# Gate projections of two branch stages: seven products of quarter blocks for eight, with sums of token quarters made during the second silu pass

## The chip, the cores and the metric

One core of a Trainium2 chip runs the whole program. The metric is the device time of one execution in microseconds. Five engines work side by side, each with its own instruction stream, ordered by semaphores only: TensorE (PE, matmuls from SBUF into PSUM), VectorE (DVE), ScalarE (ACT), GpSimd (POOL) and SyncE (SP, which here issues nearly all DMAs, in order). PSUM has eight banks of 128 x 512 floats.

## The reference, cut to what matters

The program is a two-layer hybrid block followed by a second block, on 1024 tokens of width 1024, all in float32. The change touches one part of the second block: in each of its two branches an output `o` is multiplied by a silu, projected, and gated by a sigmoid. All four factors but `o` are columns of one projection `h @ w_in`.

```python
h = rms_norm(x, norm_pre[i])
(aq, ak, av, az, dq, dk, dv, db, da, dz, gate_att, gate_dn) = split_cols(h @ w_in[i])
...
y_att = (o_att * jax.nn.silu(az)) @ w_br_att[i]
...
y_dn = (o_dn * jax.nn.silu(dz)) @ w_br_dn[i]
mix = (jax.nn.sigmoid(gate_att) * y_att + jax.nn.sigmoid(gate_dn) * y_dn) @ w_out[i]
```

`h` is 1024 x 1024; `az`, `dz`, `gate_att` and `gate_dn` are 1024 columns each; the branch weights and `w_out` are 1024 x 1024.

## The kernel before, in words

`stage_branch` (line 2653) computes one branch and is called twice: stage a for attention (tiles named `bhsa`, `bringa`, ...) and stage n for the delta branch (`bhsn`, ...). Everything is held transposed, features on the 128 partitions: `hT` as eight chunks of 128 features x 1024 tokens, in DRAM as `hTd`.

Float32 accuracy comes from splitting. Each operand is rounded to the PE's fast format (the high part, by ACT for weights and by DVE for `h`), the remainder is formed by POOL or DVE (the low part), and a product takes three matmuls: high x high, high x low, low x high. A 128x512 weight slice is one piece of work: it is loaded by SP into a staging tile (line 2726), rounded by ACT into a ring of four (line 2811), its low part is made by POOL (line 2840), and PE (line 2779) multiplies its four blocks of 128 columns with both halves of the tokens: eight units, one for each PSUM bank, three matmuls each.

The stage is six passes of eight pieces: two silu passes (four blocks of 128 output features each), two gate passes, two branch passes. In a pass every piece adds one chunk of 128 input features to all eight banks. In the first silu pass the chunks of `hT` are loaded into two buffers, rounded by DVE (line 2858) and completed by POOL (line 2833) into `hs`, where all of `h` stays for four passes. After a silu pass ACT takes the silu of each bank (line 2799) and DVE multiplies it into `yT` (line 2869). After a gate pass ACT writes the sigmoids straight from PSUM into `mixT` (line 2801). Before the branch passes `yT` is rounded into `hs` (DVE line 2873, POOL line 2837). After a branch pass DVE multiplies each bank with its gates (line 2897 in stage a, 2901 in stage n) and in stage n adds the other branch's result (line 2904), which SP has read into `yT` in one 4 MB DMA (line 2740). The result is stored (line 2750).

The order is written out by hand. SP loads a slice once POOL has used the staging tile three slices back; ACT rounds a slice once PE has used the ring entry four back:

```python
for n in range(DONE, SLICES):
    ...
    if n >= RING:
        wait_slice(act, n - RING)
    act.activation(ring[:, n % RING, 0, :], slice_in(n)[:, :], ACT.Copy).then_inc(s_hi, 1)
    c, kc = divmod(n - LEAD, KC)
    if 0 <= c < GATED and kc == KC - 1:
        activate(c)
```

The functions of a pass follow two pieces behind the rounding (`LEAD`). The first piece of each stage (and in stage n the raw inputs of the second) is prepared by the stage before. During the last branch pass stage a prepares inputs of the conv stage (`conv`), and stage n those of the last projection (`ahead`).

## Time and profile before

| | |
|---|---|
| median of 3 runs | 3266.35 us (3263.31 to 3268.9) |
| profiled execution | 3268.52 us |
| its span, first to last instruction | 3266.7 us |
| mean granted clock of TensorE | 0.971 |
| stage a | about 1746 to 2010 us of the span |
| stage n | about 2806 to 3068 us of the span |

The span is what the engines' records cover; the execution is 1.8 us longer. Busy times overlap between engines and matmuls overlap among themselves, so a matmul's mean duration is longer than the distance between two starts. The granted clock is the share of 2.4 GHz that TensorE ran at.

### The profile page before, as it was taken

How to read it: one execution, taken by the hardware profiler on the slowest of the kernel's cores; microseconds unless marked ns; L12 is line 12 of the kernel's file. 1: busy time of each engine (PE TensorE's matmuls, PEld its weight loads, DVE VectorE, ACT ScalarE, POOL GpSimd, SP SyncE). 2: the span in 40 equal slices, each digit the busy share in tenths (PEclk: the TensorE clock that was granted, in tenths of full speed). 3: DMA queues.
4: the chain of work that ended last, by engine and by line, in shares of the span. 5: the costliest groups of instructions: out<-in, count | busy, mean ns of one | idle time of the engine just before them, and what ended most of it. 6: DMA issues, size and time to landing. Idle time of an engine off the chain costs nothing. (4 is left out here: it accounts for less than half of the span.)

```text
span 3266.7 us, 43916 instructions
## 1 busy us (share of the span) xinstructions
PE 3016.7 (92%) x16017; PEld 2466.8 (76%) x16017; DVE 2044.6 (63%) x3738; ACT 1408.0 (43%) x2790; POOL 1175.9 (36%) x1306
## 2 busy tenths in 40 slices
PE   7999989989999899798999999997989888999998
PEld 5678867756887667587887887787877788788787
DVE  6889976576998756676773004677857788301244
ACT  3356557224664661335663211455434553321232
POOL 5226532232363223522004242235443445524331
PEclk8999999989999999899999999999999999999999
DMA  8422333541233245410002124124241232412342
GB/s 294 136 55 84 116 107 103 166 162 51 69 97 108 93 137 168 133 52 1 1 6 90 51 62 144 29 53 99 71 123 39 65 94 76 163 47 102 116 155 71
DMA packets 229609, 309.41 MB, mean 95 GB/s; under 512 B 41199, under 2 KB 142447, under 8 KB 227217
## 3 DMA queue, kind: packets, MB, share of 16 engines
q1 hardware_dynamic: 217874, 285.62, 28.7%
q10 hardware_dynamic: 11520, 20.98, 1.8%
q8 instruction: 128, 2.10, 0.3%
q14 instruction: 87, 0.71, 0.1%
HBM read 244.01 MB, written 62.52 MB: 94 GB/s over the span
## 5 line engine op out<-in xcount | busy, mean ns | idle before, releaser
L1027 PE MATMUL psum<-qs,hT 128*128 128x512 f32 x1248 | 284.5, 389 | 1.4 <-POOL qs L1112 1.4
L1027 PEld LDWEIGHTS psum<-qs,hT 128*128 128x128 f32 x1248 | 233.8, 188 | 51.8 <-POOL qs L1112 3.5
L2779 PE MATMUL psum<-bhsn,bringn 128*128 128x512 f32 x1056 | 241.1, 390 | 2.4 <-DVE bhsn L2861 1.5
L2779 PE MATMUL psum<-bhsa,bringa 128*128 128x512 f32 x1056 | 240.1, 389 | 2.9 <-POOL bringa L2840 2.9
L2779 PEld LDWEIGHTS psum<-bhsn,bringn 128*128 128x128 f32 x1056 | 197.9, 188 | 45.2 <-DVE bmixn L2901 2.2
L2779 PEld LDWEIGHTS psum<-bhsa,bringa 128*128 128x128 f32 x1056 | 198.1, 188 | 44.4 <-issue 3.3
L3158 PE MATMUL psum<-hTs,cws 128*128 128x512 f32 x960 | 230.2, 396 | 0.0
L3158 PEld LDWEIGHTS psum<-hTs,cws 128*128 128x128 f32 x960 | 179.3, 190 | 36.3
L1192 DVE TENSOR_SCALAR_CACHE_REDUCE junk<-score,cand 128x384 uint8<-128x384 f32 x248 | 186.8, 810 | 2.2
L1907 PE MATMUL psum<-w_out,oys 128*128 128x512 f32 x768 | 181.1, 398 | 6.9 <-POOL oys L1974 4.7
L1907 PEld LDWEIGHTS psum<-w_out,oys 128*128 128x128 f32 x768 | 147.1, 192 | 41.1 <-POOL oys L1974 5.9
L3521 DVE SCALAR_TENSOR_TENSOR cacc<-craw,taps,cacc 128x1024 f32<-128x1024 f32 x96 | 159.0, 1657 | 3.4
L1074 ACT ACTIVATE sign<-key,wbias 128x896 bf16<-128x896 f32 x124 | 134.4, 1085 | 54.8 <-POOL wbias L1118 45.2
L2202 PE MATMUL psum<-fw,fhs 128*128 128x512 f32 x552 | 135.3, 405 | 17.5 <-DVE fhs L2301 10.5
L2202 PEld LDWEIGHTS psum<-fw,fhs 128*128 128x128 f32 x552 | 106.3, 195 | 43.4 <-DVE fhs L2301 10.7
L1654 DVE CUSTOM_DVE_ANT_0 pm<-psum,score 128x384 f32<-128x384 f32 (+5 forms) x96 | 85.0, 887 | 60.1 <-PE psum L1438 45.3
L2840 POOL TENSOR_TENSOR bringa<-bstga,bringa 128x512 fp32r<-128x512 f32 x47 | 63.6, 1357 | 141.9 <-ACT bringa L2811 141.9
L2533 DVE TENSOR_REDUCE amx<-psum 128x1 f32<-128x1024 f32 x64 | 78.3, 1224 | 57.2 <-PE psum L2404 57.2
L1527 ACT ACTIVATE pm<-pm,mn 128x384 f32<-128x384 f32 (+7 forms) x128 | 99.1, 774 | 29.9 <-DVE mn L1654 29.5
L1112 POOL TENSOR_TENSOR qs<-stg,qs 128x512 fp32r<-128x512 f32 x72 | 98.8, 1385 | 34.2 <-ACT qs L1048 30.9
L2840 POOL TENSOR_TENSOR bringn<-bstgn,bringn 128x512 fp32r<-128x512 f32 x46 | 60.3, 1315 | 140.8 <-ACT bringn L2811 140.8
L1438 PE MATMUL psum<-ks,qs 128*128 128x512 f32 (+3 forms) x384 | 104.6, 384 | 4.6 <-DVE mn L1654 4.3
(564 smaller groups left out, 7134.0 us busy)
## 6 DMA issues: line engine op xcount, KB each, us to landing
stg<-in_w_in SPq DMA_DIRECT2D x88, 256.0 KB, 2.7
score<-in_w_ada SPq DMA_DIRECT2D x32, 512.0 KB, 4.3
pj<-ptmp ACTq DMA_DIRECT2D x64, 256.0 KB, 2.1
dlb<-blocks SPq DMA_DIRECT2D x32, 512.0 KB
dlb<-in_w_in SPq DMA_DIRECT2D x20, 512.0 KB, 3.9
wa<-in_w_ada SPq DMA_DIRECT2D x8, 1024.0 KB, 12.7
ostg<-in_w_out SPq DMA_DIRECT2D x16, 512.0 KB, 6.0
x<-ozb SPq DMA_DIRECT2D x16, 512.0 KB, 3.0
```

Of the source, the lines that this page charges most:

```text
L1027: mm = pe.matmul(bank(m), lhs, rhs, start=(first and x == 0), stop=(last and x == 2))
L1074: act.activation(sign[:, wide[b]], key[:, wide[b]], ACT.Sign, bias=wbias[:, b:b + 1], accum_out=wcnt[:, b:b + 1]).then_inc(s_cnt[b], 1)
L1112: pool.tensor_tensor(dst[:, 1, :], stg[n % STAGING][:, :], dst[:, 0, :].bitcast(F32), ALU.subtract).then_inc(s_lo, 1)
L1192: ins = dve.tensor_scalar(junk[:, SC_OFF[b]:SC_OFF[b + 1]], spans[b], s1, 0.0, op, ALU.add, accum_out=cnt[:, b:b + 1])
L1438: mm = pe.matmul(ps[:, 2 * (n % 2) + c // HALF, 0:m], h.qs[:, hd, i * P:(i + 1) * P], h.ks[:, x, c:c + m], start=(x == 0), stop=(x == 1))
L1527: act.activation(pm[n % PM][:, 0:keys], pm[n % PM][:, 0:keys], ACT.Exp, bias=mn[:, n:n + 1], scale=-1.0, accum_out=rs[:, n:n + 1]).then_in ...
L1907: mm = pe.matmul(ps[:, 2 * (n % SLOTS) + half, :], ys[n % YS][:, a, kc, :], w[:, b, kc, half * HALF:(half + 1) * HALF], start=(kc == 0 and ...
L2202: mm = pe.matmul(ps[:, 2 + u % 3, :], hs[n % 2][:, i, kc, :], w[c][:, j, kc, :], start=(kc == 0 and x == 0), stop=(kc == KC - 1 and x == 2))
L2779: mm = pe.matmul(ps[:, m, :], w[:, a, fs], h, start=(j == 0 and x == 0), stop=(j == KC - 1 and x == 2))
L2840: pool.tensor_tensor(ring[:, n % RING, 1, :], slice_in(n)[:, :], ring[:, n % RING, 0, :].bitcast(F32), ALU.subtract).then_inc(s_lo, 1)
L3158: mm = pe.matmul(ps[:, u % 4, :], w, h, start=(kc == 0 and x == 0), stop=(kc == KC - 1 and x == 2))
L3521: link(dve.scalar_tensor_tensor(acc[:, :], r[:, s:s + SEQ], taps[:, c, s:s + 1], acc[:, :], ALU.mult, ALU.add))
```

## The change

In the four passes that project gate columns (two in each stage), the work is cut into four pairs of 128-column blocks. For one pair, the weights form a 2 x 2 arrangement: feature half (chunks 0 to 3, chunks 4 to 7) by block; `a11` and `a21` are the first half's two blocks, `a12` and `a22` the second half's. `h` forms another: feature half by token half, `b11`, `b12` (first feature half, early and late tokens), `b21`, `b22`. Instead of eight products of quarters, seven are made:

| product | weights | tokens | bank |
|---|---|---|---|
| A11 | a11 | b11 | x |
| S2 | a21 + a22 - a11 | T2 = b22 - T1 | y |
| S1 | a21 + a22 | T1 = b12 - b11 | z |
| A12 | a12 | b21 | x, added |
| S3 | a11 - a21 | T3 = b22 - b12 | y, added |
| S4 | a12 - (a21 + a22 - a11) | b22 | z, added |
| A22 | a22 | T4 = b21 - T2 | w |

Each product is four chunks x three matmuls of 128x128 weights with 512 tokens, all into one bank. The results of a pair are A11 + A12; A11 + S2 + S1 + S4; A11 + S2 + S3 + S1; and A11 + S2 + S3 + A22. ACT copies A11 and S1 out of PSUM while they are still to be added to (`keep`), DVE makes the sums, ACT takes the sigmoids.

What goes with it:
- DVE forms the weight sums of a pair from raw weights (three after the third product's sums of the pair before, one after S2). SP loads a pair as two DMAs of 512 KB; ACT and POOL split each of the seven 128x512 weights as before, in the same ring of four.
- The token sums T1 to T4 are made in the second silu pass, for chunks i and i + 4 together, in four rounds. `hTd` is read again (eight chunks, 512 KB each). DVE makes four differences, ACT rounds three parts, DVE makes the low parts. T2 is written over the late half of chunk i in `hs`. The first pair waits for the fourth round (`s_T`).
- The gates no longer go to `mixT`, whose place T1 and T3 take: each pair's four tiles are stored to a DRAM tensor `gated` (256 KB each), and the whole is read back into `mixT` as one 4 MB DMA at the start of the branch passes, issued behind the fifth branch slice. The first multiplication waits for it (`s_gl`).
- Four `hT` buffers for two, two silu tiles for three. Chunk 0 is now loaded and split into `hs` too. Slice staging shares memory with the raw pairs.
- In stage a the three loads for `conv` get buffers of their own, without the wait between the second and the third.

The diff, cut to its core:

```diff
+    HK, PROD, PAIRS = KC // 2, 7, 4
+    RING, STAGING, LEAD, TMP, U, HST = 4, 3, 2, 2, 8, 4
+    PAIR0, BR0 = 2 * KC, 2 * KC + PROD * PAIRS
...
+    F_A11, F_S2, F_S1, F_A12, F_S3, F_S4, F_A22 = range(PROD)
...
+            def load_pair(j):
...
+                if j == 1:
+                    sp.wait_ge(s_lo, PAIR0 - DONE)
+                if j >= 2:
+                    sp.wait_ge(s_lo, item(j - 2, PROD - 1) + 1 - DONE)
+                for half in range(2):
+                    sp.dma_start(pair_raw(j)[:, half].rearrange("p k f q -> p k (f q)"),
+                                 win[:, HK * half:HK * (half + 1), columns_of(j):columns_of(j) + 2 * P]
+                                 ).then_inc(s_k[(j + 1) % 2], 16)
+            def store_gates(j):
+                for i, tl in enumerate((0, 1, 2, 3)):
+                    f, half = home(j, i)
+                    sp.wait_ge(s_out, 4 * j + i + 1)
+                    sp.dma_start(t["gated"][:, f, half * HALF:(half + 1) * HALF], tile[j % 2][tl][:, :]
+                                 ).then_inc(s_gst[j % 2], 16)
...
+            for n, i in ((KC + 1, 0), (KC + 3, 1), (KC + 4, 2), (KC + 5, 3)):
+                for v in range(KC + 2 if i == 1 else n, n + 1):
+                    load_silu(v)
+                if i == 2:
+                    load_pair(0)
+                for kc in (i, i + HK):
+                    load_chunk(chunk(kc, True))
+            for n in range(KC + 6, PAIR0):
+                load_silu(n)
+            load_pair(1)
+            load_pair(2)
+            store_gates(0)
+            load_pair(3)
+            store_gates(1)
+            for n in range(BR0, ITEMS):
+                c, kc = pass_of(n)
+                if n == BR0:
+                    sp.wait_ge(s_lo, item(PAIRS - 2, PROD - 1) + 1 - DONE)
+                if n >= BR0 + STAGING:
+                    sp.wait_ge(s_lo, n - STAGING + 1 - DONE)
+                load_slice(n, wbr[:, kc, (c - 2) * HALF:(c - 1) * HALF])
+                if n == BR0 + STAGING - 1:
+                    store_gates(PAIRS - 2)
+                if n == BR0 + STAGING + 1:
+                    store_gates(PAIRS - 1)
+                    sp.wait_ge(s_prod, PROD * PAIRS)
+                    for q in range(2):
+                        sp.wait_ge(s_gst[q], 128)
+                    sp.dma_start(mixT[:, :, :], t["gated"]).then_inc(s_gl, 16)
...
+            def product(n):
+                j, p = pair_of(n)
+                x, y, z, w = (4 * (j % 2) + i for i in range(4))
+                bank = {F_A11: x, F_S2: y, F_S1: z, F_A12: x, F_S3: y, F_S4: z, F_A22: w}[p]
+                opens = p in (F_A11, F_S2, F_S1, F_A22)
+                pe.wait_ge(s_lo, n + 1 - DONE)
+                if j == 0 and p == F_A11:
+                    pe.wait_ge(s_T, HK)
...
+                if p == F_A12:
+                    pe.wait_ge(s_kept, 2 * j + 1)
+                if p == F_S3:
+                    pe.wait_ge(s_u, 5 * j + 1)
+                if p == F_S4:
+                    pe.wait_ge(s_kept, 2 * j + 2)
+                for kc in range(HK):
+                    for i, (a, b) in enumerate(((0, 0), (0, 1), (1, 0))):
+                        mm = pe.matmul(ps[:, bank, :], ring[:, n % RING, a, kc * P:(kc + 1) * P], moving(p, b, kc),
+                                       start=(opens and kc == 0 and i == 0), stop=(kc == HK - 1 and i == 2),
+                                       skip_group_check=True)
+                mm.then_inc(s_prod, 1)
...
+            def t_hi(i):
+                a, b = hst[chunk(i, True) % HST], hst[chunk(i + HK, True) % HST]
+                act.wait_ge(s_traw, i + 1)
+                wait_item(act, KC + i)
+                act.activation(T13[:, 0, i, :], a[:, :], ACT.Copy)
+                act.activation(T4[:, 0, i, :], b[:, 0:HALF], ACT.Copy)
+                act.activation(hs[:, 0, i, HALF:SEQ], b[:, HALF:SEQ], ACT.Copy).then_inc(s_thi, 1)
...
+            def keep(j, p):
+                act.wait_ge(s_prod, PROD * j + p + 1)
+                if p == F_A11:
+                    if j == 0:
+                        act.wait_ge(s_T, HK)
+                    wait_tiles(act, j)
...
+            def activate(j, i):
+                act.wait_ge(s_u, 5 * j + 2 + i)
+                if i == 0:
+                    act.wait_ge(s_prod, PROD * j + F_A12 + 1)
+                src = ps[:, 4 * (j % 2), :] if i == 0 else tile[j % 2][i][:, :]
+                act.activation(tile[j % 2][i][:, :], src, ACT.Sigmoid).then_inc(s_out, 1)
+            def after(n):
+                j, p = pair_of(n)
+                if p in (F_A11, F_S1):
+                    keep(j, p)
+                if p == F_S3:
+                    activate(j, 0)
+                    activate(j, 1)
+                if p == F_S4:
+                    activate(j, 2)
+                if p == F_A22:
+                    activate(j, 3)
...
+            for n in range(DONE, ITEMS):
+                hi(n)
+                if KC + RING <= n < PAIR0:
+                    t_hi(n - KC - RING)
+                if n in (KC - 1 + LEAD, PAIR0 - 1 + LEAD):
+                    for m in range(U):
+                        silu(U * (n // KC - 1) + m)
+                if PAIR0 <= n - LEAD < BR0:
+                    after(n - LEAD)
...
+            def make_t(i):
+                a, b = wait_chunk(dve, i, True), wait_chunk(dve, i + HK, True)
+                early, late = slice(0, HALF), slice(HALF, SEQ)
+                link(dve.tensor_tensor(a[:, early], a[:, late], a[:, early], ALU.subtract))
+                link(dve.tensor_tensor(a[:, late], b[:, late], a[:, late], ALU.subtract))
+                link(dve.tensor_tensor(b[:, late], b[:, late], a[:, early], ALU.subtract))
+                dve.tensor_tensor(b[:, early], b[:, early], b[:, late], ALU.subtract).then_inc(s_traw, 1)
+                dve.wait_ge(s_thi, i + 1)
+                dve.tensor_tensor(T13[:, 1, i, :], a[:, :], T13[:, 0, i, :].bitcast(F32), ALU.subtract)
+                dve.tensor_tensor(T4[:, 1, i, :], b[:, early], T4[:, 0, i, :].bitcast(F32), ALU.subtract)
+                dve.tensor_tensor(hs[:, 1, i, late], b[:, late], hs[:, 0, i, late].bitcast(F32),
+                                  ALU.subtract).then_inc(s_T, 1)
+            def weight_sums(j):
+                r = pair_raw(j)
+                a11, a21, a22 = r[:, 0, :, 0, :], r[:, 0, :, 1, :], r[:, 1, :, 1, :]
+                dve.wait_ge(s_k[(j + 1) % 2], 32 * (j // 2 + 1))
+                if j:
+                    dve.wait_ge(s_lo, item(j - 1, F_S4) + 1 - DONE)
+                dve.tensor_tensor(S[0][:, :, :], a21, a22, ALU.add).then_inc(s_S, 1)
+                dve.wait_ge(s_S, 4 * j + 1)
+                dve.tensor_tensor(S[1][:, :, :], S[0][:, :, :], a11, ALU.subtract).then_inc(s_S, 1)
+                dve.tensor_tensor(a21, a11, a21, ALU.subtract).then_inc(s_S, 1)
+            def last_weight_sum(j):
+                dve.wait_ge(s_lo, item(j, F_S2) + 1 - DONE)
+                dve.tensor_tensor(S[1][:, :, :], pair_raw(j)[:, 1, :, 0, :], S[1][:, :, :], ALU.subtract).then_inc(s_S, 1)
...
+            def after_second(j):
+                tl, y = tile[j % 2], ps[:, 4 * (j % 2) + 1, :]
+                dve.wait_ge(s_prod, PROD * j + F_S2 + 1)
+                dve.wait_ge(s_kept, 2 * j + 1)
+                wait_tiles(dve, j)
+                dve.tensor_tensor(tl[2][:, :], y, tl[0][:, :], ALU.add).then_inc(s_u, 1)
+            def after_third(j):
+                tl, y = tile[j % 2], ps[:, 4 * (j % 2) + 1, :]
+                dve.wait_ge(s_prod, PROD * j + F_S3 + 1)
+                dve.tensor_tensor(tl[3][:, :], y, tl[0][:, :], ALU.add).then_inc(s_u, 1)
+                dve.wait_ge(s_kept, 2 * j + 2)
+                dve.wait_ge(s_u, 5 * j + 2)
+                dve.tensor_tensor(tl[1][:, :], tl[3][:, :], tl[1][:, :], ALU.add).then_inc(s_u, 1)
+            def after_last(j):
+                tl, z, w = tile[j % 2], ps[:, 4 * (j % 2) + 2, :], ps[:, 4 * (j % 2) + 3, :]
+                dve.wait_ge(s_prod, PROD * j + F_S4 + 1)
+                dve.tensor_tensor(tl[2][:, :], z, tl[2][:, :], ALU.add).then_inc(s_u, 1)
+                dve.wait_ge(s_prod, PROD * j + F_A22 + 1)
+                dve.tensor_tensor(tl[3][:, :], w, tl[3][:, :], ALU.add).then_inc(s_u, 1)
...
+            for kc in range(DONE, KC):
+                h_hi(kc)
+            a = wait_chunk(dve, 0)
+            dve.wait_ge(s_used, DONE)
+            link(dve.tensor_copy(hs[:, 0, 0, :], a[:, :]))
+            dve.tensor_tensor(hs[:, 1, 0, :], a[:, :], hs[:, 0, 0, :].bitcast(F32), ALU.subtract).then_inc(s_h0, 1)
+            silus(range(U))
+            for i in range(HK):
+                make_t(i)
+                if i == 1:
+                    weight_sums(0)
+            silus(range(U, 2 * U))
+            for j in range(PAIRS):
+                after_second(j)
+                last_weight_sum(j)
+                if j == PAIRS - 1:
+                    dve.wait_ge(s_sm, 2 * U)
+                    dve.wait_ge(s_prod, PROD * j + F_S2 + 1)
+                    for kc in range(HK):
+                        y_hi(kc)
+                after_third(j)
+                if j + 1 < PAIRS:
+                    weight_sums(j + 1)
+                after_last(j)
+            for kc in range(HK, KC):
+                y_hi(kc)
```

## Rows read from the trace of the kernel before

**Rows 1.** page, busy time of the engines over the whole span.

```profile
PE 3016.7 (92%) x16017; PEld 2466.8 (76%) x16017; DVE 2044.6 (63%) x3738; ACT 1408.0 (43%) x2790; POOL 1175.9 (36%) x1306
```

**Rows 2.** windows: us; PE, PEld, DVE, ACT, POOL busy; clock; DMA; GB/s.

```profile
1792.30:1835.80 43.50, 43.50 (x193) 36.02 (x193) 5.43 (x9) 9.62 (x17) 10.28 (x8) 1.00 0.19 49
1835.80:1879.30 43.50, 43.50 (x193) 36.02 (x193) 1.81 (x3) 10.88 (x18) 10.29 (x8) 1.00 0.19 49
...
2933.90:2977.40 43.50, 43.50 (x194) 36.03 (x193) 4.86 (x7) 9.60 (x17) 17.39 (x11) 1.00 0.18 49
```

**Rows 3.** timeline, first gate pass of stage a: start us, us, engine, line.

```profile
1841.53 38.24 PE L2779 MATMUL psum<-bhsa,bringa 128*128 128x512 f32 x168
...
1847.22 0.63 ACT L2811 ACTIVATE bringa<-bstga 128x512 fp32r<-128x512 f32 x1 [4.81 <-PE psum L2779]
1847.93 1.29 POOL L2840 TENSOR_TENSOR bringa<-bstga,bringa 128x512 fp32r<-128x512 f32 x1 [4.14 <-ACT bringa L2811]
```

**Rows 4.** timeline, PE in the conv stage, 24 matmuls to a bank.

```profile
2054.19 11.05 PE L3158 MATMUL psum<-hTs,cws 128*128 128x512 f32 x48
```

**Rows 5.** groups, stage a: count | busy us, mean ns | idle before it.

```profile
L2869 DVE TENSOR_TENSOR attT<-attT,btmpa 128x512 f32<-128x512 f32 x16 | 10.9, 693 | 53.4 <-ACT btmpa L2799 53.4
...
L2892 DVE TENSOR_TENSOR ahead_w<-bhsta,ahead_w 128x1024 fp32r<-128x1024 f32 x2 | 2.5, 1226 | 0.1
...
L2811 ACT ACTIVATE bringa<-bstga 128x512 fp32r<-128x512 f32 x47 | 29.2, 631 | 177.5 <-PE psum L2779 140.4 <-DMA bstga<-in_w_in 29.3 <-DMA bstga<-in_w_br_att 7.8
...
L3311 ACT ACTIVATE hTs<-ahead_h 128x2048 fp32r<-128x2048 f32 x1 | 1.9, 1917 | 23.8 <-PEq L124 23.8
...
L2799 ACT ACT_TABLE_LOAD x1 | 1.3, 1283 | 0.0
...
L2840 POOL TENSOR_TENSOR bringa<-bstga,bringa 128x512 fp32r<-128x512 f32 x16 | 20.6, 1292 | 61.7 <-ACT bringa L2811 61.7
...
L2837 POOL TENSOR_TENSOR bhsa<-attT,bhsa 128x1024 fp32r<-128x1024 f32 x3 | 7.2, 2406 | 0.0
```

**Rows 6.** timeline, end of stage n's first branch pass.

```profile
3016.71 0.69 DVE L2901 TENSOR_TENSOR bmixn<-psum,bmixn 128x512 f32<-128x512 f32 x1 [38.07 <-PE psum L2779]
3016.80 1.29 POOL L2840 TENSOR_TENSOR bringn<-bstgn,bringn 128x512 fp32r<-128x512 f32 x1 [1.97 <-ACT bringn L2811]
3017.43 1.20 DVE L2904 TENSOR_TENSOR bmixn<-bmixn,odT 128x512 f32<-128x512 f32 x1
```

**Rows 7.** page, DMA issues: count, KB each, median us to landing.

```profile
dlb<-in_w_in SPq DMA_DIRECT2D x20, 512.0 KB, 3.9
...
bstga<-in_w_in SPq DMA_DIRECT2D x31, 256.0 KB, 2.7
...
bhsta<-hTd SPq DMA_DIRECT2D x8, 512.0 KB, 3.6
...
od<-dodT SPq DMA_DIRECT2D x16, 256.0 KB, 2.5
...
odT<-mixd SPq DMA_DIRECT2D x1, 4096.0 KB, 12.2
```

**Rows 8.** timeline, stage n: the 4 MB read, the slice behind it rounded.

```profile
2998.71 0.33 SPq L2740 DMA_DIRECT2D odT<-mixd  x1
...
3011.58 1.31 ACT L2811 ACTIVATE bringn<-bstgn 128x512 fp32r<-128x512 f32 x2 [11.18 <-DMA bstgn<-in_w_br_dn]
```

**Rows 9.** timeline, PE in stage n: a pass starts; after waiting for DVE.

```profile
2934.23 0.39 PE L2779 MATMUL psum<-next_bh_hi,bringn 128*128 128x512 f32 x1
...
3027.63 39.06 PE L2779 MATMUL psum<-bhsn,bringn 128*128 128x512 f32 x171 [0.37 <-DVE bmixn L2901]
```

**Rows 10.** timeline, PE after a gap: stage a; the stage behind n.

```profile
1754.37 38.36 PE L2779 MATMUL psum<-bhsa,bringa 128*128 128x512 f32 x168 [2.91 <-POOL bringa L2840]
...
3070.27 11.94 PE L4456 MATMUL psum<-mw,mms 128*128 128x512 f32 x44 [3.58 <-PEq L2666]
```

**Rows 11.** windows, the 4 us behind that gap.

```profile
3070.00:3074.00 4.00, 3.73 (x10) 3.01 (x11) 0.00 (x0) 0.97 (x2) 0.50 (x2) 0.57 0.60 196
```

More of the change, by code:

```diff
@@ L2723, in _ @@
-                off = {"silu": silu_off, "gate": gate_off, "branch": 0}[what]
-                off += part * HALF
-                src = (wbr if what == "branch" else win)[:, kc, off:off + HALF]
-                sp.dma_start(stg[n % STAGING][:, :], src).then_inc(s_w[n % STAGING], 16)
-                if c == 0 and y_in is not None and kc >= HG:
-                    for f in range(2 * (kc - HG), 2 * (kc - HG) + 2):
-                        sp.dma_start(yT[:, f, :], y_in[:, f, :]).then_inc(s_y[f // 4], 16)
@@ new lines, in _ @@
+            for n in range(LOADED, KC):
+                if y_in is not None and n == HG:
+                    sp.wait_ge(k.od_last[0], 32)
+                    sp.wait_ge(k.od_last[1], 32)
+                load_chunk(chunk(n, False))
+                load_silu(n)
+                if y_in is not None and n >= HG:
+                    for f in range(2 * (n - HG), 2 * (n - HG) + 2):
+                        sp.dma_start(yT[:, f, :], y_in[:, f, :]).then_inc(s_y[f // 4], 16)
+            load_chunk(chunk(0, False))
@@ L2738, in _ @@
+                if conv and c == 3 and kc == 3:
+                    sp.dma_start(hst[2][:, :], t["hTd"][:, 0, :]).then_inc(s_chi, 16)
+                if mix_in is not None and c == 2 and kc == KC - 1:
                     sp.wait_ge(s_ylo, KC)
```

323 lines of the change are left out of this document (207 added, 116 removed).

## The prediction

> **What bounds the kernel now.** I read the page's busy line first: TensorE (PE) is busy for 92% of the span, no other engine over 63% [rows 1]. That is an average, so I went to the windows, one for each pass of the two branch stages (called a and n here, after the tag in their tile names). In each of the four gate passes and in stage a's second silu pass PE is busy for the whole 43.50 us, at a granted clock of 1.00, while VectorE (DVE), ScalarE (ACT) and GpSimd (POOL) are busy for 2 to 17 us and the DMA share is 0.17 to 0.19 (the silu pass, the first and the last gate pass are shown) [rows 2]. Then the timeline of one gate pass: ACT's roundings come 5.44 us apart (4.81 of waiting for PE and 0.63), and POOL's low part follows at once; the two feeders wait for PE, never PE for them [rows 3]. So here a matmul saved is time saved, as long as the feeders keep their lead. The price of a matmul is the spacing of starts and not the mean of 389 ns, which overlaps: 43.50 us / 192 = 0.2266 us.
>
> **The matmuls.** A gate pass is 8 pieces x 8 units x 3 = 192 matmuls; two stages with two passes each make 768. After: 2 stages x 4 pairs x 7 products x 12 = 672, all with the same 128x128 weights and 512 moving columns. Removed: 96 x 0.2266 = 21.75 us, on the path. What is new is that twelve follow each other in one PSUM bank, where before three did. The conv stage does just that (24 in a row): 48 in 11.05 us, less the 0.39 of the last, over 47 gaps: 0.227 us [rows 4]. Cost nothing; bounds 0 and, if each of the 56 products paid the 0.16 us between 0.39 and 0.227 once for a drain, 9 us. I take 0: pieces follow each other today with a wait between them and no gap: 168 in 38.24 us [rows 3].
>
> **Feeding the pairs.** A product lasts 12 x 0.2266 = 2.72 us, a pair 19.03. Per pair POOL has 7 x 1.29 = 9.0 us, ACT 7 roundings, two copies and four sigmoids at 0.63, 8.2 us, DVE nine operations at 0.69, 6.2 us [rows 3, 5]. All are below 19, so only the order can hurt. Counted from the pair's start, the products end at 2.7, 5.4, 8.2, 10.9, 13.6, 16.3, 19.0. The tight place is the next pair's first two weights. DVE ends its two sums after the third sum's product (S3) at 15.1; ACT, whose two sigmoids wait for them, ends those at 15.8 and rounds the next A11 by 16.4; POOL has the low part at 17.8, needed at 19.0. For the next product DVE must first pass three weight sums (to 17.3) and the sum of S4 (18.0), then ACT a sigmoid and a rounding (19.35), POOL a low part (20.7), needed at 21.8: 1.1 us in hand. The third product's weight comes at 22.5, needed at 24.5. In a two-input DVE operation on SBUF that meets a POOL one the row is 1.20 us for 0.69 [rows 6], and one such meeting falls into the three sums: 0.6 left. Stall 0; bounds 0 and, with all five DVE operations at 1.20, 2.55 - 1.1 = 1.5 us at each of the six inner boundaries, 9 us. I take 0.
>
> In those same rows DVE starts at 3017.43 inside POOL's 3016.80 to 3018.09 and ends 0.54 us after it, so here the later one seems to wait until the other is through. The Trainium skill (SBUF — State Buffer, Who interferes with whom) says so as a rule: such an operation and a GpSimd read take one shared port in turn and the second "fully blocks". By it the third weight sum would wait for the whole of POOL's 1.29 us, the weight would come at 21.85 for 21.8, and the sum would be 0.6 us longer over six boundaries.
>
> **The quarter sums in the second silu pass.** Counted from its start. DVE forms four differences (2.95 us with their links), ACT rounds three parts (1.06 + 0.63 + 0.63, the first taken between the 0.63 for 512 and the 1.92 for 2048 elements), DVE takes three low parts (1.23 + 0.69 + 0.69) [rows 5]: 7.9 us per chunk pair, four in a chain, beside which PE works on. Round one cannot end before ACT's rounding may overwrite chunk 0 (5.44): 11.1. SP then has chunk 2 queued behind that round, and behind chunk 2 slice 13, which ACT rounds before its part of round two: 512 KB twice and 256 KB, by rows of 3.6 and 2.7 us about 5 us [rows 7], so round two ends at 21.8; three weight sums to 24; rounds three and four at 32.6 and 40.5. Needed at 43.5: 3 us in hand, with slices 13, 14 and 15 ready 9, 4 and 6 us before use. The second silu products on DVE start 1.7 us late behind it, and the weight of the third product is ready at 47.3 for 48.9. Cost 0.25 us per stage as an even guess between none and a small slip; bounds 0 and 3 us per stage.
>
> **SP's queue.** Per stage sixteen slices go; nine chunk reads (512 KB), eight half-pair loads (512 KB), sixteen gate stores (256 KB) and one 4 MB read-back come, all in order. A pair is asked for 20 us or more before its sums, against 3.9 us for a 512 KB weight load [rows 7]; the DMA share of 0.19 leaves room. The stores wait for sigmoids of the pair just ended, and what stands behind them (the next pair but one) isn't due for more than 14 us. The read-back is the exception. Count from the branch pass's start: the last stores go out at 2.4 (behind slice 4, which waits for POOL's second low part) to 4.0, land 2.5 later [rows 7], the read starts at 6.4. The same size and layout exists today as the read of mixd in stage n: issued 2998.71, and the slice queued behind it reaches ACT at 3011.58, 12.9 us later [rows 8]. So slice 5 is rounded at 19.9, its low part there at 21.3, needed at 27.2; the gates are there at 19, the first multiplication comes at 39.0 (3016.71 [rows 6], less the pass's start: the pass before starts at 2934.23 [rows 9], and 43.5 later is 2977.7). Hidden, by 5.9 and 20 us.
>
> In stage n the mixd read stands behind it. It is released by POOL's low part of y chunk 7: after slice 5's 21.3 come 2.40, 1.29 and 2.40, so 27.4, against 21.0 now [rows 5, 8]. It lands at 39.6 to 40.2 (12.2 to 12.9 later), and the first addition wants it at 39.7 (multiplication at 39.0 plus 0.69) [rows 6, 7]. DVE is the path there already: its pairs of 1.35 us hold PE up by 1.5 us before the last unit (due 43.5 + 4.8 after 2977.7, started 3027.63; the 171 that it opens run on without a gap) [rows 9]. So each us of lateness counts in full. The value is 0.4 us, from the landing in the middle or a little late; bounds 0 and 3.
>
> **Start and end of the stages.** The first chunk and slice are issued in the same order; stage a's wait of 2.91 us for POOL [rows 10] stays, since the chain cast, low part, low part is the same. Four hT buffers for two change nothing there. The sigmoid table load (1.28 us) [rows 5] moves to the first pair, where ACT has 4 us free between its seventh rounding (10.0) and the first sigmoid (14.4).
>
> **Sum.** -21.75 + 2 x 0.25 + 0.4 = -20.9 us. The profiled execution took 3268.52 us (span 3266.7 and 1.8 around it), 2.17 above the median of the runs, 3266.35. So 3247.6 for a like execution, 3245.4 as a median.
>
> **Rivals.**
> 1. The hand-over at the pair's end becomes the path (DVE, ACT and POOL in a row). For: 0.6 us in hand, six times, and DVE slows beside POOL. Against: they are idle for more than half of a pair. 9 us given back: 3254.
> 2. The quarter sums come late. For: four rounds in series, each over three engines and one over DMA. Against: 3 us in hand. 3 us beyond it per stage: 3251.
> 3. The other side, slower: the big reads. If 4 MB takes d more than 12.9 us, stage a stalls for d - 5.9 at slice 5 and stage n for 2d + 0.4, both reads being in series before its additions. It decides at d = 9 (22 us for one read): 3 + 18.4 gives back the 20.9. At double time, d = 12.9, the price is 7 + 26, so about 3278. For: the gate rows were only just written, and slices run beside. Against: the same layout took 12.2 us to land [rows 7].
> 4. No change: the saving is eaten at every product (0.39 us x 56 = 21.8), if each product's start waited for its weight in full: 3266. Against: a ring of four weights and POOL at half load.
>
> **Chances.** Forecast 0.65, rival 1 0.15, rival 2 0.10, rival 3 0.05, rival 4 0.05. About 0.2% (6.5 us) is what a measurement can tell from no change. The forecast and rivals 1 and 2 are faster by more: 0.90; rival 4 is within it, 0.05; rival 3 slower, 0.05. The range reaches down 4 us for the unknown costs at zero and the spread of the runs, and up to rival 1 with 3 us more: 3241 to 3257.
>
> **What would show it.** Right: the gate stretch of each stage takes 76.1 us for 87.0, at clock 1.00 with PE busy throughout; no PE idle at a pair's start; PE's only new wait is for the first addition in stage n. Rival 1: PE idle before products 1 to 3 of a pair, released by POOL. Rival 2: PE idle at the first product, released by DVE's low parts. Rival 3: PE idle in the branch pass, ACT released by DMA. The clock matters if a gap grows: after 3.58 us without a matmul the granted clock was 0.57 in the next 4 us, that is 1.2 GHz for most of it [rows 10, 11]. Wrong altogether would be a gate stretch shorter than 76 us or matmuls spaced wider than 0.2266 us.

## The result, and the profile after

The changed kernel takes 3248.11 us (median of 4 runs, 3247.25 to 3252.7) against 3265.35 us for the kernel before on the same chip (4 runs, 3263.31 to 3268.9): a ratio of 0.995 [0.9937, 0.9962], 17.2 us less. The forecast was 20.9 us less, 3245.4 us, with a range of 3241 to 3257 that holds the time. The profiled execution takes 3248.78 us, its span 3247.0. Its busy line, from the page, answers to [rows 1]:

```profile
PE 3000.5 (92%) x15921; PEld 2452.1 (76%) x15921; DVE 2169.6 (67%) x3870; ACT 1442.8 (44%) x2854; POOL 1225.1 (38%) x1330
```

PE has 96 matmuls fewer, as counted, and DVE 132 operations more. The share of PE is 92% as before and says nothing. So I cut the span where a stage's first matmul starts and where the first of the stage behind it does. This gives a table, and the stage times of all runs below are taken the same way (us; "rest" is from stage n's end to the end of the span; the clock is the one granted in the 4 us behind stage a's first gap):

| execution | stage a | between | stage n | rest | clock |
|---|---|---|---|---|---|
| before | 267.39 | 792.57 | 264.54 | 196.43 | 1.00 |
| before, profiled again (before_again) | 268.81 | 794.87 | 264.39 | 196.38 | 0.61 |
| changed | 259.04 | 791.04 | 258.41 | 195.30 | 0.65 |
| changed, profiled again (again) | 257.39 | 792.63 | 258.51 | 197.34 | 1.00 |

Ahead of stage a the code is the same, yet that stretch scatters over 8 us (1739 to 1747), "between" and "rest" by 4 and 2. Outside the two stages the first profile of the changed kernel took 5.2 us less than that of the kernel before, but the unaltered kernel, profiled again, took 4.2 less there too. Single spans are therefore compared by stage. The 96 matmuls make 10.88 us per stage. Stage a gives 10.0 of them where both clocks are 1.00 and 8.35 in the first pair; stage n gives 6.1 and 6.0.

**The pairs.** Windows of the four pairs, stage a and then n; the columns are those of [rows 2]:

```profile
1835.20:1912.40 77.20, 76.44 (x337) 62.98 (x336) 28.95 (x44) 33.45 (x58) 40.17 (x29) 1.00 0.24 79
2878.10:2955.40 77.30, 76.46 (x335) 62.63 (x335) 29.19 (x44) 33.47 (x58) 39.56 (x29) 1.00 0.24 79
```

Two passes of 43.50 us [rows 2] became one stretch of 77.25 in stage a (1835.16 to 1912.41) and of 77.83 in n (2878.16 to 2955.99), for 76.1 forecast. What is above is mostly one gap. It is in the timeline of PE, stage a first, then n:

```profile
1835.16 5.63 PE L2928 MATMUL psum<-bhsa,bringa 128*128 128x512 f32 x24
1841.56 3.02 PE L2928 MATMUL psum<-bt13a,bringa 128*128 128x512 f32 x12 [0.76 <-POOL bringa L3062]
1844.41 2.88 PE L2928 MATMUL psum<-bhsa,bringa 128*128 128x512 f32 x12
...
2884.69 3.02 PE L2928 MATMUL psum<-bt13n,bringn 128*128 128x512 f32 x12 [0.84 <-POOL bringn L3062]
```

Both times it is the third product of the first pair that waits for POOL's low part. With the slower matmuls around the gap (3.02 us for the twelve behind it, not 2.88) the fourth product starts 1.09 us late in stage a and 1.23 in n: due were 1843.32 and 2886.32, three products of 2.72 us after the pair's start, and it came at 1844.41 and 2887.55. No other product of either stage waits; the pairs' boundaries show nothing. A product starts 2.72 us after the other (1844.41 and the next, 1847.13), twelve to one bank or not.

**The quarter sums.** Stage a's silu pass starts at 1791.64. Timeline, all engines, what leads up to that gap:

```profile
1803.67 0.43 SPq L2785 DMA_DIRECT2D braw0a<-in_w_in  x1
...
1808.41 0.63 ACT L2984 ACTIVATE bringa<-braw0a 128x512 fp32r<-128x512 f32 x1 [8.08 <-DMA braw0a<-in_w_in]
1808.95 1.04 ACT L2990 ACTIVATE bt13a<-bhsta 128x1024 fp32r<-128x1024 f32 x1
...
1812.81 0.68 DVE L3103 TENSOR_TENSOR bhsa<-bhsta,bhsa 128x512 fp32r<-128x512 f32 x1
...
1817.51 0.69 DVE L3099 TENSOR_TENSOR bhsta<-bhsta 128x512 f32<-128x512 f32 x1
1819.14 0.63 ACT L2984 ACTIVATE bringa<-braw0a 128x512 fp32r<-128x512 f32 x1 [8.11 <-DMA braw0a<-in_w_in]
...
1822.94 1.78 DVE L3102 TENSOR_TENSOR bt4a<-bhsta,bt4a 128x512 fp32r<-128x512 f32 x1
1824.64 0.68 DVE L3103 TENSOR_TENSOR bhsa<-bhsta,bhsa 128x512 fp32r<-128x512 f32 x1
...
1831.41 1.78 DVE L3102 TENSOR_TENSOR bt4a<-bhsta,bt4a 128x512 fp32r<-128x512 f32 x1
...
1833.12 1.77 DVE L3103 TENSOR_TENSOR bhsa<-bhsta,bhsa 128x512 fp32r<-128x512 f32 x1
1834.81 5.53 DVE L3126 TENSOR_TENSOR attT<-attT,btmpa 128x512 f32<-128x512 f32 x8
1839.52 0.62 ACT L2984 ACTIVATE bringa<-bsum0a 128x512 fp32r<-128x512 f32 x1
1840.22 1.28 POOL L3062 TENSOR_TENSOR bringa<-bsum0a,bringa 128x512 fp32r<-128x512 f32 x1 [5.88 <-ACT bringa L2984]
```

Read it backwards. The weight comes last from POOL, after ACT's rounding, after ACT's silus for the eight products of DVE, and these products begin when DVE's last low part of round four ends at 1834.89. That is 43.25 us into the pass, where the forecast had 40.5.

Now forwards. ACT's part of round two waits behind slice 13 (8.08 us of idle time), but the forecast had counted this wait: the round ends at 1813.49, 21.85 us into the pass for 21.8. The loss comes after it. In round three DVE's differences are done at 1818.20, and ACT first waits for slice 14 until 1819.14 and rounds it. Then one low part of DVE in round three and two in round four meet POOL's work and take 1.78, 1.78 and 1.77 us for 0.69. Round three ends at 1825.32, 33.7 us in for 32.6, and round four 2.75 us late.

**Stage n's first branch pass** (PE starts it at 2955.99):

```profile
2964.32 0.32 SPq L2863 DMA_DIRECT2D bmixn<-gated  x1
...
2977.27 0.63 ACT L2984 ACTIVATE bringn<-braw1n 128x512 fp32r<-128x512 f32 x1 [14.91 <-DMA braw1n<-in_w_br_dn]
...
2985.28 0.33 SPq L2873 DMA_DIRECT2D odT<-mixd  x1
...
2995.06 0.69 DVE L3212 TENSOR_TENSOR bmixn<-psum,bmixn 128x512 f32<-128x512 f32 x1 [31.21 <-PE psum L2965]
2997.55 0.69 DVE L3215 TENSOR_TENSOR bmixn<-bmixn,odT 128x512 f32<-128x512 f32 x1 [1.80 <-DMA odT<-mixd]
2998.15 1.94 ACT L2984 ACTIVATE bringn<-braw1n 128x512 fp32r<-128x512 f32 x3 [18.77 <-DMA braw1n<-in_w_br_dn]
2998.86 6.35 POOL L3062 TENSOR_TENSOR bringn<-braw1n,bringn 128x512 fp32r<-128x512 f32 x4 [12.35 <-ACT bringn L2984]
2998.88 1.82 DVE L3215 TENSOR_TENSOR bmixn<-bmixn,odT 128x512 f32<-128x512 f32 x1
...
3000.20 2.34 PE L2965 MATMUL psum<-bhsn,bringn 128*128 128x512 f32 x9 [0.49 <-POOL bringn L3062]
...
3009.06 39.06 PE L2965 MATMUL psum<-bhsn,bringn 128*128 128x512 f32 x171 [0.36 <-DVE bmixn L3212]
```

The read of mixd is issued 29.3 us into the pass (before: 21.0), its data hold up DVE's first addition for 1.80 us, and that moves the additions among four low parts of POOL: the second addition takes 1.82 us instead of 0.69. Six short gaps of PE follow. Five of them (0.51, 0.72, 0.71, 0.36, 0.36) are waits for DVE; the first, 0.49, is one for POOL. It has the same origin: the slices queued behind the late read reach ACT at 2998.15, and POOL's low part for the second pass is ready at 3000.2, when PE was due to start on it at 2999.5. The last unit starts 4.8 us after its due time, 2955.99 + 48.3, where it had 1.6 before (due 3026.0, started 3027.63 [rows 9]).

### The profile page after: what moved, and what is told of

Read it like the earlier page. It is cut to its first block and busy times, and to the rows that moved or that the text cites. A ratio compares the mean times of both kernels' runs of the same rounds, so it can differ in the third digit from the quotient of the medians.

```text
span 3247.0 us, 44116 instructions
## 1 busy us (share of the span) xinstructions
PE 3000.5 (92%) x15921; PEld 2452.1 (76%) x15921; DVE 2169.6 (67%) x3870; ACT 1442.8 (44%) x2854; POOL 1225.1 (38%) x1330
## 5 line engine op out<-in xcount | busy, mean ns | idle before, releaser
L2965 PE MATMUL psum<-bhsn,bringn 128*128 128x512 f32 x744 | 170.9, 390 | 4.6 <-DVE bmixn L3212 2.7
L2965 PE MATMUL psum<-bhsa,bringa 128*128 128x512 f32 x744 | 170.7, 392 | 2.9 <-POOL bringa L3062 2.9
L2965 PEld LDWEIGHTS psum<-bhsn,bringn 128*128 128x128 f32 x744 | 139.1, 188 | 36.3 <-DVE bmixn L3212 4.8
L2965 PEld LDWEIGHTS psum<-bhsa,bringa 128*128 128x128 f32 x744 | 140.7, 189 | 32.7 <-issue 3.3
L3764 POOL TENSOR_TENSOR cws<-dlb,cws 128x1024 fp32r<-128x1024 f32 x20 | 63.0, 3156 | 120.9 <-ACT cws L3619 120.9
L1542 ACT ACTIVATE pT<-psum 128x512 f32<-128x512 f32 (+3 forms) x192 | 86.0, 485 | 46.8 <-PE psum L1446 46.6
```

What stands on the lines that cost most here:

```text
L1542: act.activation(pT[v % 2][:, part[0]:part[0] + m, n % 2, n % GH // 2, :], src[:, 0:m], ACT.Copy).then_inc(s_pT, 1)
L2965: mm = pe.matmul(ps[:, m, :], w[:, a, fs], h, start=(j == 0 and x == 0), stop=(j == KC - 1 and x == 2))
```

## The experiments

Open were four questions: why stage a gave 8.35 us and not 10.6; what makes the third product wait; what stage n lost beside that (the late read, POOL beside the additions, the address of a buffer); and whether the price of a matmul and of the change by stage is what I took. All ratios are to the kernel before, timed on the same chip in the same rounds.

**The two kernels once more** (again and before_again, unaltered).

> The changed kernel once more, unaltered, as the yardstick of this set. In the first profile the two changed stages took 259.0 us (stage a) and 258.4 us (stage n) for 267.4 and 264.5 before, 14.5 us less, while the span fell by 19.7: 5.2 us came from code that is the same in both. Theory A: those 5.2 us are scatter between executions (when the PE's clock is granted after a gap), so here the rest of the program takes another time than in that profile, by a microsecond or more in one place or another, and the 1.75 us that stage a lost to a lower clock right after its first gap (granted clock 0.65 over 4 us, 1.00 before the change at the same place) need not return. Theory B: the changed stages leave the rest in a better state, and the 5.2 us and the 1.75 us return as they were. Both: 3248 +- 2 us median.

> The kernel before, once more, for its trace. Ratio 1.000 within the interval. Theory A (scatter of the clock after gaps): stage a and stage n take 267.4 and 264.5 us again unless the clock falls after stage a's first gap of 2.9 us (then 1.5 to 2 us more in stage a, also in this kernel); the other stretches scatter by 1 to 3 us. Theory B (the lower clock in stage a belongs to the change): the granted clock after that gap is 1.00 again and in every trace of a kernel with the old stages.

Measured: again 3250.74 us, 12.9 less than the kernel before in its rounds, 0.9964 [0.9951, 0.9977]; before_again 3265.4 us, 0.9999 [0.9991, 1.0008]. Stage a's first matmuls in the changed kernel, from the timelines of the first profile and of "again":

```profile
1751.83 83.50 PE L2965 MATMUL psum<-bhsa,bringa 128*128 128x512 f32 x360 [2.94 <-POOL bringa L3062]
```

```profile
1748.63 81.89 PE L2965 MATMUL psum<-bhsa,bringa 128*128 128x512 f32 x360 [2.89 <-POOL bringa L3062]
```

The same 360 matmuls behind the same gap take 1.61 us more in the first. The windows say why: the 4 us behind it, in the first profile, and the same 4 us in before_again:

```profile
1751.80:1755.80 4.00, 3.97 (x12) 3.13 (x13) 2.59 (x2) 1.08 (x2) 4.00 (x2) 0.65 0.62 211
```

```profile
1747.95:1751.95 4.00, 4.00 (x11) 3.17 (x12) 0.91 (x1) 0.63 (x1) 4.00 (x3) 0.61 0.63 202
```

Granted was 0.65 of full speed, in part 1.2 GHz, after an idle PE of 2.94 us; in "again" it stayed at 1.00. The old stage a has it too (0.61). So stage a's missing 1.6 us in the first pair are scatter and no effect of the change. The same goes for what was gained outside the stages: t_order, below, has the same code there as the changed kernel, and its profile takes 0.2 us less there than the first one of the kernel before, not 5.2.

A median of these runs scatters by a few microseconds. The intervals below are good for telling a kernel from the kernel before; those of t_order, split and both overlap with that of "again", and what such an edit is worth is read from its own stretch of the timeline.

**The quarter sums' order** (t_order). Rounds three and four are queued behind one slice more each on SP:

```
-for n, i in ((KC + 1, 0), (KC + 3, 1), (KC + 4, 2), (KC + 5, 3)):
-    for v in range(KC + 2 if i == 1 else n, n + 1):
+for n, i in ((KC + 1, 0), (KC + 3, 1), (KC + 5, 2), (KC + 6, 3)):
+    for v in range({1: KC + 2, 2: KC + 4}.get(i, n), n + 1):
...
-for n in range(KC + 6, PAIR0):
+for n in range(KC + 7, PAIR0):
```

> Slices 13 and 14 of the second silu pass are asked for before the token chunks of the third and fourth round, not behind them; nothing else changes. Theory A (the quarter sums are late, because ACT rounds its part of a round only behind a slice that SP asks for behind the round before): the second and third rounds start about 3 us and 1 us sooner, the fourth ends near 40 us into the pass for 43.2, DVE takes up its silu products when ACT delivers the first, and the gap of 0.76 us (a) and 0.84 us (n) before the third product goes: 1.6 us faster than the changed kernel. Theory B (two silu tiles for three make ACT wait for DVE at each unit, whatever DVE did before): the rounds end sooner, the gaps stay within 0.2 us of what they are, and the time stays.

Measured: 3244.37 us, 0.9946 [0.9932, 0.9959]. Timeline and window of stage a:

```profile
1815.63 0.68 DVE L3103 TENSOR_TENSOR bhsa<-bhsta,bhsa 128x512 fp32r<-128x512 f32 x1
...
1826.04 0.68 DVE L3103 TENSOR_TENSOR bhsa<-bhsta,bhsa 128x512 fp32r<-128x512 f32 x1
...
1832.80 1.78 DVE L3102 TENSOR_TENSOR bt4a<-bhsta,bt4a 128x512 fp32r<-128x512 f32 x1
...
1834.51 1.78 DVE L3103 TENSOR_TENSOR bhsa<-bhsta,bhsa 128x512 fp32r<-128x512 f32 x1
1836.21 5.54 DVE L3126 TENSOR_TENSOR attT<-attT,btmpa 128x512 f32<-128x512 f32 x8
```

```profile
1839.00:1916.50 77.50, 77.50 (x343) 64.19 (x342) 27.93 (x42) 31.96 (x57) 40.76 (x29) 1.00 0.24 82
```

The pass starts at 1795.72. Rounds two, three and four end 20.6, 31.0 and 40.6 us into it (1816.31, 1826.72, 1836.29), and PE is busy for the whole of the window: the pairs take 76.16 us (1839.24 to 1915.40), those of stage n 76.60. Stage n is down to 257.10. Rounds that don't wait behind a slice remove the gap; Theory B is out. But the low parts beside POOL are as slow as before (1.78 twice in round four). So the order of the slices is the cure, and what had been left out of the forecast is still there: that 40.6 meets its 40.5 is luck. The forecast had counted a wait for slice 13 that is gone here, and not the meetings with POOL that are here.

**The read-back in pieces** (split): eight reads of 512 KB behind the branch slices 4 to 6 instead of one of 4 MB, so that slice 5 and then the mixd read go earlier.

```
-sp.dma_start(mixT[:, :, :], t["gated"]).then_inc(s_gl, 16)
+for f in {4: (0, 1), 5: (2, 3, 4), 6: (5, 6, 7)}.get(n - BR0, ()):
+    sp.dma_start(mixT[:, f, :], t["gated"][:, f, :]).then_inc(s_gl, 16)
...
-dve.wait_ge(s_gl, 16)
+dve.wait_ge(s_gl, 128)
```

> The gates are read back in eight parts of 512 KB, two behind the fifth branch slice, three behind the sixth and three behind the seventh, instead of one 4 MB read behind the fifth. Theory A (order in SP's queue: the sixth slice waits out the 4 MB, POOL stands in line for its low part with the y chunks behind it, and so the mixd read of stage n is asked for 29.3 us into the pass): slice 5 is rounded before 18 us for 21.3, the mixd read is asked for at about 25 us, the first addition doesn't wait (1.80 us now), POOL has fewer low parts to make up for beside DVE's additions, and the last unit of the next pass starts 2 to 3 us sooner. Stage a stays as it is. 2 to 3 us faster than the changed kernel. Theory B (8 MB and the slices simply take this long, in any order): the mixd read lands as late as now, 41.5 us into the pass, and the time stays.

Measured: 3245.24 us, 0.9954 [0.9938, 0.9969]; stage n 256.40, 2.1 less. Timeline (the pass starts at 2953.4):

```profile
2967.99 0.63 ACT L2985 ACTIVATE bringn<-braw1n 128x512 fp32r<-128x512 f32 x1 [8.19 <-DMA braw1n<-in_w_br_dn]
2977.96 0.32 SPq L2874 DMA_DIRECT2D odT<-mixd  x1
...
2993.18 1.53 DVE L3216 TENSOR_TENSOR bmixn<-bmixn,odT 128x512 f32<-128x512 f32 x1
...
3004.39 39.06 PE L2966 MATMUL psum<-bhsn,bringn 128*128 128x512 f32 x171 [0.36 <-DVE bmixn L3213]
```

Slice 5 is rounded 14.6 us into the pass for 21.3. Issued 24.6 us in, the mixd read no longer holds up an addition, and PE's wait for POOL is gone too. The additions themselves, some of them beside POOL (1.53 us for the first), still start the last unit late, by 2.7 us.

**Both** edits together.

> The two edits together. Theory A: they sit in different places, both on the path, so the gains add: 3.6 to 4.6 us faster than the changed kernel, about 3244 us. Theory B for either: what that edit gave alone, and no more.

Measured: 3245.33 us, 0.9947 [0.9935, 0.996]; stage n 255.23, 1.2 less than split alone and 3.2 less than the changed kernel. Stage a took 259.01 at a granted clock of 0.50 behind its gap, so its part doesn't show in the stage's time; it shows in the pairs, which take 76.16 us (1837.96 to 1914.12).

**The additions out of the way** (late_add): in stage n DVE only multiplies the first eight units, which is all that PE waits for, and makes their eight additions before the ninth unit.

```
+dve.wait_ge(s_in, 16)
+for v in range(U):
+    at = slice((v % 2) * HALF, (v % 2 + 1) * HALF)
+    dve.tensor_tensor(mixT[:, v // 2, at], mixT[:, v // 2, at], yT[:, v // 2, at], ALU.add).then_inc(s_add, 1)
...
-dve.wait_ge(s_in, 16)
+if u < U:
+    continue
```

> In stage n DVE makes all eight multiplications of the first branch pass first, and then the eight additions of the other branch; in the changed kernel each multiplication waits behind the addition before it. Nothing else changes: the gates are read back in one 4 MB DMA, and the mixd read lands as late as there. Theory A (the late read cost time only because the first addition stood in front of the multiplications that PE waits for): no wait of PE for DVE at the next pass's units, which follow the multiplications 0.68 us apart; stage n 4 to 4.8 us shorter (3.3 us that the change added and the 1.5 us that were there before), with only the 0.5 us for POOL's low part left. Theory B (POOL's low parts and DVE's work slow each other whatever the order, and the slices behind the read are late): 2 us or less.

Measured: 3246.26 us, 0.9938 [0.9926, 0.995]; stage n 254.24, 4.2 less. PE's one wait left in the branch passes:

```profile
2999.51 43.86 PE L2965 MATMUL psum<-bhsn,bringn 128*128 128x512 f32 x192 [0.69 <-POOL bringn L3062]
```

It is the wait for the slices behind the late read, which this edit leaves as it was. From the branch pass's start (2955.10) to the stage's end stage n takes 91.85 us for 95.71, so the additions between the units were worth 3.9 us net of that wait; 1.6 of it the kernel before has too [rows 9]. The other 0.3 us lie in the first pair, where the gap was 0.61 us for 0.84 with the same code.

**Twelve matmuls more in each pair** (eight): the twelve of product A22 are issued twice, so the four pairs have the 384 matmuls that two passes had, with all else of the change in place. The second twelve start the bank anew and write the same product over the first.

```
-for kc in range(HK):
+for again in range(2 if p == F_A22 else 1):
+    for kc in range(HK):
```

> The last product of each pair is computed twice, the second time over the first: twelve matmuls more per pair, eight products' worth of work for seven, with all the rest of the change (sums, stores, reads) in place. Theory A (a matmul on this path costs its spacing, and the rest of the change costs only what its gaps cost): the stretch of the four pairs takes 77.2 + 4 x 2.72 = 88.1 us in each stage, the program 21.8 us more than the changed kernel, about 4 us more than the kernel before. Theory B (the shorter stretch has brought another limit close, so that part of the matmuls' time was already cover for the feeders): less than 18 us more, and the gap before the third product is gone with it.

Measured: 3267.1 us, 1.0011 [1.0001, 1.0022]: 16 to 19 us above the two medians of the changed kernel (3250.74 and 3248.11, from other rounds) and not below the kernel before. Stage a has 270.00, 10.9 more than the first profile of the changed kernel at a like clock (0.67 and 0.65), as 48 x 0.2266 = 10.88 wants. Stage n has 267.15, only 8.7 more, though its pairs too are 11.1 us longer. Its branch pass starts at 2981.06 and is 2.3 us shorter to the stage's end (93.37 us for 95.71). The timeline shows where:

```profile
3006.97 0.33 SPq L2873 DMA_DIRECT2D odT<-mixd  x1
...
3020.85 0.69 DVE L3216 TENSOR_TENSOR bmixn<-bmixn,odT 128x512 f32<-128x512 f32 x1
```

With longer pairs the read is issued 25.9 us into the pass and nothing waits for it. The gates' read ahead of it goes out at 5.1 us for 8.3. So I put 2.3 us of the late read's price down to the pairs being faster: what the reads wait for is ready no sooner, and the pass that they are due in starts sooner.

**One stage alone** (new_a, new_n): the other stage calls the old function.

> Stage a as changed, stage n as before. Theory A (each stage's gain is its 48 matmuls less its own gaps, and the rest of the program only scatters): stage a 257.4 us (259 if the clock falls after its first gap), stage n 264.5; 10.0 us faster than the kernel before, ratio 0.997. Theory B (the stretches outside gained through the change): the sum of the rest falls too, and the ratio is 0.996 or less.

> Stage n as changed, stage a as before. Theory A: stage a 267.4 us (269 with the lower clock), stage n 258.5, with the gap before the third product and the waits for DVE's additions as in the changed kernel; 6.0 us faster than the kernel before, ratio 0.998. Theory B (the late mixd read comes from stage a's part of the change, for instance from what it leaves in DRAM or in the queue): stage n 255 to 256 us here.

Measured: new_a 3255.58 us, 0.9966 [0.9955, 0.9977], 10.1 us less; new_n 3263.01 us, 0.9988 [0.9978, 0.9997], 2.7 less with an interval of 1.0 to 7.2, whose upper part holds the 6 of the stage table. In new_n's profile stage n has 259.87, 1.4 more than in the changed kernel, and the same late read:

```profile
3000.03 0.33 SPq L3130 DMA_DIRECT2D odT<-mixd  x1
...
3012.35 0.69 DVE L3472 TENSOR_TENSOR bmixn<-bmixn,odT 128x512 f32<-128x512 f32 x1 [2.89 <-DMA odT<-mixd]
```

PE's wait for POOL behind it is 1.57 us here, where it was 0.49; with the same code in stage n it was 1.25 in off_a. The two gains add up to the whole within what the intervals hold, and stage n's loss is its own, not handed over from a.

**Where T4 lies** (align, off_a). Stage n's matmuls on bt4n took 396 ns at the median in the changed kernel, all others 389. Its buffers are put at the top of SBUF, at an address that is 32 above a multiple of 64 bytes. align moves them down by 32 bytes; off_a moves stage a's, which lie on a multiple, up by 32.

```
-park = nc.sbuf_top
+park = nc.sbuf_top - nc.sbuf_top % LINE      (align, stage n)
-park = nc.sbuf_base
+park = nc.sbuf_base + 32                     (off_a, stage a)
-k.sb(ctx, "bpark", [P, 2 * KC * HALF])
+k.sb(ctx, "bpark", [P, 2 * KC * HALF + 16])
```

> The changed kernel with one edit: in stage n the fourth token sum (and what lies behind it) is moved down by 32 bytes, to a start that is a multiple of 64. Theory A (the place of the moving operand costs: in stage n these matmuls take 396 ns at the median for 389 elsewhere, and a product 2.80 us for 2.72): 389 ns in all four products of stage n, the stretch of its pairs 0.34 us shorter. Theory B (another cause, such as what DVE and POOL do beside these products): 396 ns stays.

> The reverse: in stage a, whose fourth sum starts at a multiple of 64 and whose matmuls take 389 ns, it is moved up by 32 bytes. Theory A: 396 ns and 2.80 us for the last product of each pair in stage a as well. Theory B: 389 ns stays in stage a.

Measured, one run each: 3246.98 and 3247.94 us, beside 3263.69 for the kernel before. The groups (duration ns min/median/max) of align in stage n and off_a in stage a:

```profile
L2929 PE MATMUL psum<-bt4n,bringn x48: 389/389/389, 2892.0 to 2951.6; 128*128 128x512 f32 x48
```

```profile
L2928 PE MATMUL psum<-bt4a,bringa x48: 393/396/399, 1849.4 to 1909.5; 128*128 128x512 f32 x48
```

The 7 ns come and go with the address. In the changed kernel they make a pair of stage n 19.16 us long (2898.51 to 2917.67) and one of stage a 19.04 (1855.29 to 1874.33): 0.12 us, 0.48 over four pairs. In align a pair of stage n takes 19.04 us (2894.75 to 2913.79), and in off_a one of stage a takes 19.16 (1852.24 to 1871.40). The stage's time doesn't show it: 257.87 us in align, 257.65 in off_a, where stage n is unaltered.

**The best of it** (best: t_order, split, late_add and align together).

> The earlier slices, the divided gate read and the late additions together, and the fourth token sum's tile moved by 32 bytes so that it starts at a multiple of 64. Theory A: stage a as in the run with the earlier slices (256.1 us when the clock does not fall after its first gap, 1.8 more when it does); stage n has neither the gap before the third product nor a wait for DVE, 253.0 us for 258.5; the matmuls on the fourth sum take 389 ns for 396 if it is the place that costs. 6 to 7 us faster than the changed kernel, about 3242 us. Theory B: the read of mixd, now ahead of the time at which it is needed, leaves only what the earlier slices gave: 1.6 us.

Measured: 3241.96 us (3238.44 to 3247.34), 0.9929 [0.9917, 0.9941]: 22.8 us below the kernel before, and faster than the changed kernel as "again" (0.9951 or more); against the first set of runs the intervals overlap (0.9937 to 0.9941). Stage n takes 251.77, 12.8 less than before, and PE waits in it only at its start. Its timeline, the first silu passes and a product on T4:

```profile
2796.98 81.88 PE L2967 MATMUL psum<-bhsn,bringn 128*128 128x512 f32 x360 [1.48 <-DVE bhsn L3091]
...
2895.01 2.88 PE L2930 MATMUL psum<-bt4n,bringn 128*128 128x512 f32 x12
```

## Why the prediction was right, and where it was not

- **The matmuls, -21.75 us: right.** Without the gap the pairs take 76.16 us for 87.0. "eight" shows the price from the other side: 10.9 us in stage a for 48. Twelve to one bank cost nothing.
- **Feeding the pairs, 0 in 0 to 9: right.** No boundary of the six has a gap; rival 1 is out. The 0.6 us in hand were not tried by any run. (The prediction's working for a whole wait there has a slip: 20.7 and 1.29 make 22.0 and not 21.85, over 1 us for six boundaries and not 0.6. Neither shows at a boundary.)
- **The quarter sums, 0.25 us per stage: the place right, the size too small.** 1.09 and 1.23 us. What failed is the price of rounds three and four, 7.9 us each and a little. The ends of rounds one and two came as forecast, the wait for slice 13 included (21.85 us for 21.8). But I had priced DVE's low parts alone, 0.69 us, though I had charged a meeting with POOL at the pairs' boundaries; three of them took some 1.78, which is 3.3 us, and round three also waited for slice 14. So round four ended at 43.25 and not at 40.5, and of the 1.6 us that the third product's weight had in hand nothing was left. By the signs that I had set down this gap, at the third product and released by POOL, reads as rival 1; the chain behind it is rival 2's, at some 40% of its price of 3 us.
- **The read-back, hidden: right.** 12.95 us from its issue to the next slice's rounding for 12.9 forecast, and in stage a PE has no gap in the branch passes (384 matmuls in 87.20 us). Rival 3 is out. But it was issued 8.3 us into stage n's pass for my 6.4.
- **The mixd read behind it, 0.4 us in 0 to 3: this term was mis-sized.** It came to 3.2 us, at the last unit (4.8 for 1.6; my 1.5 there was a slip) as at the stage's end (95.71 us from the pass's start for 92.54). The first addition was late by 1.8 us and not by 0.4: ahead of the first read DVE's four copies of y chunks and POOL's low parts ran into each other (1.75 and 2.85 us of POOL for 1.29 and 2.40). I let lateness count one for one, leaving out what DVE finds when it starts late: POOL's four low parts, so that 0.69 became 1.82. And I left out the slices that stand behind the read in SP's queue, for which PE waited 0.5 us itself. split takes these waits away and brings 2.1 us; late_add, which leaves the wait for POOL, brings 3.9, of which 1.6 are the old ones.
- **Stage n's matmuls on T4, 0.48 us: not foreseen.**
- **Start and end, 0: right for stage a** (2.94 us of waiting for 2.91); in stage n the two silu passes take 84.87 us for 84.98.
- **Sum.** -21.75 + 1.09 + 1.23 + 3.2 + 0.48 = -15.8, against -10.0 and -6.0 measured in the two stages in "again", where the clock is that of the kernel before. The first pair's -19.7 (spans) holds in addition 1.6 us lost to the clock and 5.2 us gained outside the two stages, which no part of the change touches; the 4.2 us of the unaltered kernel say that this is scatter.
- **Luck.** The change is worth some 16 us and not 20.9. From 3266.35 that is 3250.5, which is rival 2's number (3251) and not the forecast's (3245.4). The two medians are 17.2 and 12.9 us less, on either side of it, and the first lies nearer the forecast by scatter. The range, 16 us wide, would have held the numbers of rivals 1 and 2 as well, so it is the timelines and the edits that tell the mechanisms apart, not the time.

The DVE operations beside POOL agree with what the Trainium skill (SBUF — State Buffer, Who interferes with whom) says of the shared port, that the second "fully blocks": 1.77 and 1.82 us for 0.69 here, where the row of before had 1.20 [rows 6]. The 1.82 end at 3000.70, some 0.55 us after POOL's first low part, whose 1.3 us began at 2998.86. At the pairs' boundaries, where I had weighed it, it cost nothing.

## What to carry over

A matmul saved on a saturated TensorE is worth its start-to-start spacing at once, but the work that prepares it and the queue behind it get less time: after costing what is removed, list for each later due time what now comes relatively earlier. In a series of small steps over three engines look for the instruction that waits for a transfer with part of the chain behind it; moving two slices forward in the queue bought back what the chain had lost. Price a chain of vector operations in the company that it will have, not at the duration of each alone, and again when it slips. And a late read is late for all that is queued behind it.

## What the runs showed of the hardware

- A moving operand of 128x512 that starts 32 bytes past a multiple of 64 made its matmul 396 ns (393 to 399) and not 389, in both stages and only there; moving it by 32 bytes switched it either way, in one run each.
- Two-input DVE operations of 0.69 us on SBUF took 1.77 to 1.82 us where they began inside a POOL operation of 1.29, and POOL's own took up to 1.81 where DVE had begun first.
- Behind stage a's first gap, of 2.8 to 3.1 us, the granted clock of the next 4 us was 1.00 in four of the fourteen profiles and 0.50 to 0.67 in ten, with the same code on either side (again and the first profile of the changed kernel). Over the 360 matmuls behind it that cost 1.3 to 2.8 us (83.18 to 84.66 for 81.89). What decides between them stays open.
- Stretches that no edit touched differ from one execution to the next by 2 to 8 us (the table's "between" and "rest", and what is ahead of stage a). An effect of a microsecond is seen in the timeline of its own stretch and not in the span.
